# One third of the columns at a time through the first normalisation, and three small reorderings behind it

## What is computed

```python
mix, st = mixer(rmsnorm(x, norm1_w), p, states)   # one input projection w_in, three mixers, gated merge, w_out
x = x + mix
xn = rmsnorm(x, norm2_w)
x = x + square(relu(xn @ w_up)) @ w_down
y = rmsnorm(x, final_norm_w)
def rmsnorm(x, w): return x * rsqrt(mean(x * x, -1) + EPS) * w
```

## Time and profile before

| | |
|---|---|
| Median of 3 runs | 2195.5 us (2195.11 to 2198.4) |
| The profiled execution | 2200.46 us, of which 2198.7 us are the span of its instructions |
| TensorE busy | 2166.3 us, 99% of the span |
| VectorE, ScalarE, GpSimd busy | 971.9, 758.2 and 571.2 us |
| DMA | 222 MB, 101 GB/s over the span |

### The profile page before, as it was taken

How to read it: one execution, slowest core, us unless ns; L and a number is a source line. 1 busy time by engine, 2 the same in 40 slices (tenths; PEclk the granted TensorE clock), 3 DMA queues, 4 the chain that set the end, 5 groups by cost and what they waited for, 6 DMA issues and landing times.

```text
span 2198.7 us, 36263 instructions
## 1 busy us (share of the span) xinstructions
PE 2166.3 (99%) x13762; PEld 2104.9 (96%) x13762; DVE 971.9 (44%) x1522; ACT 758.2 (34%) x1342; POOL 571.2 (26%) x375
## 2 busy tenths in 40 slices
PE   7999999999999999999999999999999999999998
PEld 6999999999899999899998999999999999999997
DVE  5888323333665664244445365442222222222225
ACT  5556323232465563233332333231312213122132
POOL 2438623323211212212212222212221221212120
PEclk9999999999999999999999999999999999999999
DMA  4224536442244323456431744202111111111112
GB/s 173 67 80 135 162 114 188 128 133 89 83 125 144 99 97 118 128 161 193 143 109 59 254 148 146 97 25 58 29 58 34 52 52 33 57 33 52 52 40 88
DMA packets 191538, 222.09 MB, mean 101 GB/s; under 512 B 38670, under 2 KB 146226, under 8 KB 191334
## 3 DMA queue, kind: packets, MB, share of 16 engines
q1 hardware_dynamic: 164364, 179.81, 27.0%
q10 hardware_dynamic: 27098, 41.23, 5.3%
HBM read 162.22 MB, written 58.77 MB: 101 GB/s over the span
## 4 chain that ended last, share of the span: by engine, by line
PE 79%; issue 8%; POOL 4%; DVE 4%; DMA 2%; ACT 2%; SPq 1%; ACTq 0%; POOLq 0%; DVEq 0%
PE D L432 65%; PE D L2811 2%; POOL w_lo L412 2%; POOL b_t L738 1%; POOL b_u L735 1%; DVE u_x L546 1%; PE MM L1302 1%; PE MM L1890 1%; DMA proj<-stage 0%; PE MM L2367 0%; PE MB L1974 0%; PE MM L872 0%; PE MB L2284 0%; PE D L2367 0%; PE MB L2234 0%
## 5 line engine op out<-in xcount | busy, mean ns | idle before, releaser
L432 PE MATMUL D<-xn_hi,w_hi 128*128 128x352 f32 x1992 | 663.7, 333 | 7.3 <-ACT stage L451 2.8
L412 POOL TENSOR_TENSOR w_lo<-w_raw,w_hi 128x1024 fp32r<-128x1024 f32 (+1 forms) x163 | 338.7, 2078 | 1184.7 <-ACT w_hi L406 1184.7
L432 PE MATMUL D<-xn_lo,w_hi 128*128 128x352 f32 x1992 | 644.2, 323 | 0.0
L432 PE MATMUL D<-xn_hi,w_lo 128*128 128x352 f32 x1992 | 643.9, 323 | 0.0
L432 PEld LDWEIGHTS D<-xn_hi,w_hi 128*128 128x128 f32 x1992 | 375.7, 189 | 22.5 <-issue 12.8
L432 PEld LDWEIGHTS D<-xn_lo,w_hi 128*128 128x128 f32 x1992 | 375.8, 189 | 4.7 <-issue 3.8
L432 PEld LDWEIGHTS D<-xn_hi,w_lo 128*128 128x128 f32 x1992 | 375.5, 189 | 0.0
L406 ACT ACTIVATE w_hi<-w_raw 128x1024 fp32r<-128x1024 f32 (+1 forms) x163 | 143.7, 882 | 346.8 <-PE D L432 296.4
L432 PE MATMUL D<-z_lo,w_hi 128*128 128x352 f32 x768 | 247.9, 323 | 0.0
L432 PE MATMUL D<-z_hi,w_lo 128*128 128x352 f32 x768 | 247.8, 323 | 0.0
L432 PE MATMUL D<-z_hi,w_hi 128*128 128x352 f32 x768 | 247.2, 322 | 0.0
(11 more groups left out here) (557 smaller groups left out, 3066.6 us busy)
## 6 DMA issues: line engine op xcount, KB each, us to landing
w_raw<-in_w_proj SPq DMA_DIRECT2D x73, 512.0 KB, 3.7
proj<-stage ACTq DMA_DIRECT2D x60, 528.0 KB, 3.3
w_raw<-in_w_half SPq DMA_DIRECT2D x72, 256.0 KB, 2.7
w_raw<-in_w_full SPq DMA_DIRECT2D x24, 512.0 KB, 3.6
stage<-proj SPq DMA_DIRECT2D x23, 528.0 KB, 3.6
d_bc<-rowd SPq DMA_DIRECT2D x32, 256.0 KB, 5.7
m_in<-proj SPq DMA_DIRECT2D x32, 256.0 KB, 3.8
f_w<-in_w_full SPq DMA_DIRECT2D x16, 512.0 KB, 3.5
```

What stands on the lines that cost most here:

```text
L412: nc.gpsimd.tensor_tensor(w_lo[t.slot][:, 0:kt, :], raw(t)[0][:, 0:kt * P].rearrange("p (k m) -> p k m", m=P), w_hi[t.slot][:, 0:kt, :].bi ...
L432: last = nc.tensor.matmul(D[b][:, 0:GN], w[t.slot][:, k, :], x, start=(k == 0 and n == 0), stop=(k == kt - 1 and n == 2))
```

## The change

1. `xin` comes by thirds of the columns: for each third four loads of two blocks by 352 columns (352 KB), the weights of tile 0 behind the first third, those of tile 1 behind the second. The squares go into a buffer of their own (`sqs`), 24 of 352 columns in place of 8 of 1056; 12 additions of 352 columns in place of 4 of 1056; 12 totals either way. Those of the first third come first; those of the next third stand between the pieces of this one: on ScalarE two squares behind each of the pieces 0 to 3, the root of the next third behind piece 6, the high part of tile 1's weights behind piece 2; on VectorE an addition behind each of the pieces 1 to 4; on TensorE a total behind the tile-0 matmuls of each of the pieces 2 to 5.
2. The gate rows: `ROW_SLOTS` is `[3, 6, 2, 4, 3]`, ScalarE has the first slot and its evacuations ahead of the first Exp, and evacuates once more ahead of the copies of `tok`.
3. SP into the DeltaNet loop: `stored_all` and `d_z` of chunk 0 go ahead of the `td` stores and the `d_t0`/`d_tt0` loads, and for chunk 1 the four `d_bc` go ahead of the weights of tile 19, `d_qk` and `d_v`.
4. The end: in the last block of each third VectorE adds the square of the block before ahead of the bank, and `SCALED` moves one scaling from step 6 to step 7.

```diff
-        x_ld = [sem(f"x_ld{k}") for k in range(KT)]
+        x_ld = [[sem(f"x_ld{g}{p}") for p in range(KT // 2)] for g in range(TG)]
...
+        SQ_AFTER = {k: (2 * k, 2 * k + 1) for k in range(KT // 2)}
+        ROOT_AFTER, WEIGHTS_AFTER = KT - 2, 2
+        ADD_AFTER = {k + 1: k for k in range(KT // 2)}
+        SUM_AFTER = {k + 2: k for k in range(KT // 2)}
...
+        def first_square(eng, g, k):
+
+            eng.wait_ge(x_ld[g][k // 2], 16)
+            if g:
+                eng.wait_ge(*nm_pe["1"].after(f"p{g - 1}{k // 2}"))
+            eng.activation(sqs[:, k, :], xin[:, k, gcols(g)], ACT.Square).then_inc(*nm_act["1"].step(f"q{g}{k}"))
+
+        def first_add(eng, g, p):
+
+            eng.wait_ge(*nm_act["1"].after(f"q{g}{2 * p + 1}"))
+            eng.tensor_tensor(sqs[:, 2 * p, :], sqs[:, 2 * p, :], sqs[:, 2 * p + 1, :], ALU.add).then_inc(*nm_dve["1"].step(f"a{g}{p}"))
+
+        def first_total(eng, g, p):
+
+            eng.wait_ge(*nm_dve["1"].after(f"a{g}{p}"))
+            eng.matmul(M[g][:, 0:GN], ones, sqs[:, 2 * p, :], start=p == 0, stop=p == KT // 2 - 1).then_inc(*nm_pe["1"].step(f"p{g}{p}"))
...
+                        if t == 0 and k in SUM_AFTER and g + 1 < TG:
+                            first_total(eng, g + 1, SUM_AFTER[k])
...
                 root(0)
                 for i, (g, k) in enumerate(PIECES):
-                    if i in (4, 6):
-                        root(i // 2 - 1)
                     eng.wait_ge(*dve_.after(f"s{i}"))
...
+                    if i == WEIGHTS_AFTER:
+                        make_hi(eng, Tile(1))
+                    if g + 1 < TG:
+                        for x in SQ_AFTER.get(k, ()):
+                            first_square(eng, g + 1, x)
+                        if k == ROOT_AFTER:
+                            root(g + 1)
...
                     if i:
                         low(i - 1)
+                    if k in ADD_AFTER and g + 1 < TG:
+                        first_add(eng, g + 1, ADD_AFTER[k])
...
-            for k in range(KT):
-                if k == KT // 2:
-                    load_w(sp, Tile(0), w_proj[0])
-                sp.dma_start(xin[:, k, :], xT[k]).then_inc(x_ld[k], 16)
-            load_w(sp, Tile(1), w_proj[1])
+            for g in range(TG):
+                for p in range(KT // 2):
+                    src = xT[2 * p:2 * p + 2, :, gcols(g)].rearrange("k p t -> p k t")
+                    sp.dma_start(xin[:, 2 * p:2 * p + 2, gcols(g)], src).then_inc(x_ld[g][p], 16)
+                if g < 2:
+                    load_w(sp, Tile(g), w_proj[g])
...
-        ROW_SLOTS, ML_SLOTS = [9, 2, 4, 3], [3, 3, 3, 3, 3, 3]
+        ROW_SLOTS, ML_SLOTS = [3, 6, 2, 4, 3], [3, 3, 3, 3, 3, 3]
...
             if kind == "act":
+                slot()
+                slot.evacuate()
                 eng.wait_ge(*rw_dve.after("bc"))
...
                 slot()
+                slot.evacuate()
                 eng.wait_ge(*rw_pe.after("tok"))
...
                 if n is not None:
                     gates()
                 else:
+                    stored_all(eng, GD0)
+                    gates()
                     inverse_loads(eng, 3)
                     eng.wait_ge(zeroed, 2)
...
-                if n is None:
-                    stored_all(eng, GD0)
-                    gates()
...
-            chunk_loads(sp, gdn, LOOP_GD, 0, 3)
+            gdn("sp", sp, 0, None, False, between="ahead")
+            load_w(sp, Tile(LOOP_GD + 2), w_proj[LOOP_GD + 2])
+            gdn("sp", sp, 0, lambda: load_w(sp, Tile(LOOP_GD + 3), w_proj[LOOP_GD + 3]), False, between="behind")
+            chunk_loads(sp, gdn, LOOP_GD, 1, 3)
...
-        SCALED = {3: (0,), 4: (1, 2), 5: (3, 4), 6: (5, 6), 7: (7,)}
+        SCALED = {3: (0,), 4: (1, 2), 5: (3, 4), 6: (5,), 7: (6, 7)}
...
+                    if d < KT - 1:
+                        gather()
                     if d:
                         eng.wait_ge(*act_.after(f"q{g}{d - 1}"))
...
+                    if d == KT - 1:
+                        gather()
```

More of the change, by code:

```diff
@@ L1497, in rows @@
             if kind == "pool":
-                for _ in range(4):
+                for _ in range(5):
                     slot()
             if kind == "pe":
+                slot()
                 slot()
@@ L1667, in gdn @@
                 if between != "rest":
-                    for k in range(2):
-                        eng.dma_start(hn(B.qk, k * C4), pcols(GD_TILE + 4 * (1 - k), 4, col0, N)).then_inc(gx_in if sample else gd_in, 16)
+                    if between != "ahead":
+                        for k in range(2):
+                            eng.dma_start(hn(B.qk, k * C4), pcols(GD_TILE + 4 * (1 - k), 4, col0, N)).then_inc(gx_in if sample else gd_in, 16)
                 def token_rows():
@@ L1681, in gdn @@
                         eng.wait_ge(s_, 16 * NCONV // 2)
-                eng.dma_start(hn(B.v), pcols(GD_TILE + 8, 4, col0, N)).then_inc(gx_in if sample else gd_in, 16)
-                if n is not None or sample:
+                if between != "ahead":
+                    eng.dma_start(hn(B.v), pcols(GD_TILE + 8, 4, col0, N)).then_inc(gx_in if sample else gd_in, 16)
+                if (n is not None or sample) and between != "behind":
                     prefetch(eng, None if sample else n, (gd_dve, "ge"))
@@ L1688, in gates @@
                     eng.dma_start(hn(B.z), pcols(GZ_TILE, 4, col0, N)).then_inc(gx_in if sample else gd_z, 16)
+                if between == "ahead":
+                    return
                 if sample:
@@ L2308, in build @@
                   "3": steps("nm3_dve", last_names + " " + " ".join(f"s{TG - 1}{k}" for k in range(KT)))}
[L2309 to L2330, removed]
-                    i.then_inc(*nm_pe["1"].step(f"p{pair}"))
@@ new lines, in build, with gcols @@
+        nm_pe = {"1": steps("nm1_pe", " ".join(f"p{g}{p}" for g in range(TG) for p in range(KT // 2))),
+                 "3": steps("nm3_pe", " ".join(f"s{g}" for g in range(TG)))}
+        def gcols(g):
+            return slice(g * GN, (g + 1) * GN)
+        def first_square(eng, g, k):
[3 more added lines that the diff above has]
+            eng.activation(sqs[:, k, :], xin[:, k, gcols(g)], ACT.Square).then_inc(*nm_act["1"].step(f"q{g}{k}"))
@@ L3156, in _ @@
             dve.wait_ge(*lb_act.after("ln"))
-            for k in range(KT):
-                first_sum("dve", dve, k)
-            norm_scale("dve", dve, "1", xin, nrs[:, :], (nsq[:, :], ntmp[:, :]), PC_N1)
+            for p in range(KT // 2):
+                first_add(dve, 0, p)
+            norm_scale("dve", dve)
             mix_program("dve", dve)
@@ L3172, in _ @@
             pe.wait_ge(const_ld, 32)
-            for k in range(KT):
-                first_sum("pe", pe, k)
+            for p in range(KT // 2):
+                first_total(pe, 0, p)
             mix_program("pe", pe)
```

53 lines of the change are left out of this document (31 added, 22 removed).

## The result

The changed kernel takes **2205.25 us** (median of 7 runs, 2203.24 to 2208.14), the kernel before, run beside it, 2196.35 (median of 7, 2193.69 to 2201.1): a ratio of 1.004, 95% interval 1.0031 to 1.0049, so 8.9 us slower. The forecast was 2197.0 with a range to 2201.0; the result lies 4 us above that range. The profiled execution after took 2205.49 us, close to its median. The one before took 2200.46, 4.1 above its own. Of the 8.9 us between the medians the two profiles can therefore show only 5.0, and the other 3.9 need other executions of the kernel before.

The account below looks back on a forecast made before the run. TensorE, busy 99% of the span, was taken as the bound. Start +0.8, gate rows -1.1, DeltaNet loop +1.8, clock 0 and end 0 sum to +1.5: 2202.0 in the profile's frame, 2197.0 for the median, range 2190.0 to 2201.0.

Parts of the forecast that it names:

- The start, +0.8 expected: Start by thirds: the pair of tiles 0 and 1 ends at 50.9 in place of 50.1; bounds -1.7 and +2.3.
- VectorE's two operations on a piece 0.92: Start, supply of pieces: VectorE needs 0.92 us for its two operations on each piece, from 34 in 15.56.
- an addition adds 0.46: Start, supply of pieces: VectorE's addition adds 0.46 us to four of eight pieces, 1.4 each.
- 0.50 up to the middle: Start: TensorE at half clock up to the middle of the first third, the pair then ending at 50.4.
- the bound of +1.7 in the text: Start: all of the first third at half clock, the pair ending at 51.8, +1.7.
- The gate rows, -1.1 expected: Gate rows: 0.6 of the 0.8 stall and 0.45 of the 1.6 one go; bounds 0 and -2.4.
- The stall at x5: Into the DeltaNet loop: TensorE, ready at 257.91, waits for the last load at 262.5, +4.6.
- The rival in which they issue slowly: Into the DeltaNet loop: eight loads at 1.0 us each, stall 8.3, +5.2, 2200.7 us; chance 0.20 (0.21 by range).
- so -2.8 in full: Into the DeltaNet loop: chunk 1's `d_bc` ahead removes the whole 2.8 us TensorE stall at L451.
- the clock: 0 net: Behind the new x5 stall: same half clock as behind the old stall, which lost 2.7; between -1.0 and +0.7.
- the +1.8 of the text: Into the DeltaNet loop: sum of the price +4.6 at x5 and the gain -2.8 at L451.
- I carry differences over unchanged: Frame: sums made against the profiled 2200.46 us, 5.0 above the median 2195.5, hold for the median too.

Follow-up runs that it names:

- the run with the short pieces: Start alone on the kernel before, with GpSimd's `make_lo` of tiles 0 and 1 cut into eight operations of 128 columns: 2199.39 us, ratio 1.0013.
- three kernels: Start alone on the kernel before, plus `make_lo` cut into eight operations (2199.39 us), plus fill matmuls (2201.36), or plus both (2200.36).
- the fills' kernel: Start alone on the kernel before, plus fill matmuls of 256 columns whose result nobody reads: 2201.36 us, ratio 1.0019.
- another kernel with the same fills: Kernel before plus gate rows, early `d_bc`, and the new start with both cut `make_lo` and fill matmuls: 2197.37 us, ratio 0.9996.

## Why the prediction was wrong, point by point

Two steps failed. Between the two profiles +1.5 was forecast and +5.0 measured, and the start makes 3.1 of the difference: its stream of pieces was laid out without GpSimd and with too little half clock. Between the medians another 3.9 come on top, because a stall and a fall of the clock that the profile before holds were booked as a gain in full.

**The start, +0.8 expected, +3.9 in the trace, 1.8 to 3.1 in time.** The step that failed is the one that laid out the supply of pieces. The first piece was nearly right (14.5, measured 15.34 with one lengthened scaling ahead of it). "VectorE's two operations on a piece 0.92" and "an addition adds 0.46" left out that GpSimd makes the low half of tile 1's weights in just that stretch: one addition took 2.13. From there on the stream was late: the first matmul of piece 5 came at 25.61 (21.8 laid out), the Ln of the second root at 28.26 (22.9), piece 8 at 30.36 (26.7). The kernel before already showed it in miniature. Its addition of squares takes 1.26 alone and 1.62 where it starts beside one `make_lo`, and the next `make_lo`, which starts beside that addition, takes 2.84 in place of 2.48; it was read past because nothing waited there:

```profile
8.25 1.26 DVE L2323 TENSOR_TENSOR nsq<-nsq,ntmp 128x1056 f32<-128x1056 f32 x1 [3.23 <-ACT ntmp L2320]
...
16.70 2.48 POOL L412 TENSOR_TENSOR w_lo<-w_raw,w_hi 128x1024 fp32r<-128x1024 f32 x1 [14.12 <-ACT w_hi L406]
...
18.68 1.62 DVE L2323 TENSOR_TENSOR stage<-stage 128x1056 f32<-128x1056 f32 x1 [1.72 <-ACT stage L2320]
19.68 2.84 POOL L412 TENSOR_TENSOR w_lo<-w_raw,w_hi 128x1024 fp32r<-128x1024 f32 x1 [0.49 <-ACT w_hi L406]
```

The Trainium skill (SBUF — State Buffer, SBUF: two separate sides) says that a VectorE operation with two SBUF inputs and a GpSimd operation that reads SBUF exclude each other for the whole instruction; by that rule, the trace agrees, both for the addition (18.74 to 20.87 beside 18.02 to 20.49) and for the run with the short pieces, and it should have been a term of the sum. The second half of the miss is the clock: "0.50 up to the middle" was taken and the whole first third was at 0.50, which alone was the bound of +1.7 in the text, 51.8. The two lengthened operations hold 0.85 and 1.6 us more; with both the end came to 54.01, beyond the upper bound of +2.3. The 3.9 can't be split between them: the end came 1.8 us earlier with either one taken away, and 1.4 with both.

That a thin stretch is followed by half clock was itself read from a single event. In the six other kernels with the old start the same stretch was as thin, 1.54 to 1.75 us busy of 3.50, and the clock behind it stayed at 1.00. So the fall is an event with a chance. In the kernel with SP's order alone the two stretches read:

```profile
22.60:26.10 3.50, 1.69 (x7) 1.13 (x8) 3.43 (x8) 2.16 (x5) 1.43 (x4) 1.00 0.06 22
26.10:29.50 3.40, 2.78 (x12) 1.62 (x11) 3.40 (x8) 3.09 (x8) 0.00 (x0) 1.00 0.00 0
```

**The gate rows, -1.1 expected, -1.5 in the trace.** The first stall went whole (0.8, where 0.6 was taken), the second lost 0.5 (where 0.45 was). The mechanism and its size held; in time the part alone gave 0 with an interval of 2 us either way, and with the early `d_bc` -2.6. One term was left out of the sum: the clock behind the second stall. Behind the 1.6 us stall it fell for 3.4 us in six of nine profiled executions; behind the shortened one of 1.1 us it stayed at 1.00 in all five. Step x5 came at 256.7 and 256.9 in the two kernels with the new gate rows and the old start, at 257.91 in the profile before, which has no fall there, and at 259.5 to 259.9, waits at x5 taken off, in the four that have the old start and the fall. Whether that is a gain in time isn't shown: the mean granted clock of the twelve executions with the gate rows alone (0.997) is that of the kernel before beside them.

**Into the DeltaNet loop: the price was right, the gain was not.** The stall at x5 was forecast at 4.6, from the store of tile 16 down to the last load, and measured 5.10. Two terms inside it were off and nearly cancel: the `td` stores landed after 4.2 to 4.8 (2.7 to 3.1 taken, from a trace in which they went one at a time), and the eight loads took 3.7 to issue (4.3 taken). The rival in which they issue slowly did not happen. The failed step is "so -2.8 in full", and with it "the clock: 0 net". Both were read from one execution. In the six other profiled kernels with the old order that stall was 0.7, 0.8, 1.1, 1.2, 1.5 and 2.0, and TensorE kept its clock behind it. So the change took away about 1 us there and brought 5.1, with 6.8 us at 0.50 behind it where 1.52 + 3.40 were busy: up to 2.5 lost. That sum, 5.1 + 2.5 - 1, is 6.6, against 6.4 measured for the part alone. Against the profiled execution the same rows give 5.1 + 2.5 - 2.8 - 2.7 = +2.1, so the +1.8 of the text was right in its own frame.

**The end, 0 expected, 0 measured** (1.0001).

**The frame.** "I carry differences over unchanged" is the step that cost the other 3.9. The execution profiled before stood 4.1 us above its median. It held a long stall and a fall of the clock that none of the other profiled kernels with that order had, and a change that removes them gains little against the median. The granted clocks on record bear this out. In the 98 other executions of the kernel before that ran beside the experiments the time goes with the mean granted clock: 2198.6 us on average at 0.996 (38 executions), 2196.7 at 0.997 (32), 2195.2 at 0.998 (25) and 2193.7 at 0.999 (3). The profiled one stands at 0.995, below them all; a part of that is its fall at 26 us, which cost little. All the rows that pointed at them were single events, and the distance of 5.0 between 2200.46 and 2195.5, named in the text, was the hint. In hindsight the sum would be: the profile's excess (2.8 - 1 of stall, 2.7 of clock, together 4.5) off the gain, which gives +6.0, 2201.5, and with the start as measured 2204.6.

**Open.** The lines on the start: three kernels moved the pair's end by 1.4 to 1.8 us and none moved the time by as much as the intervals can tell. Why the fills' kernel was the slowest of them isn't settled. Nor is what SP's order costs beside the rest of the change (9.7 us, and 6.4 alone), or whether the stores landed late because they were issued close together or because `d_z` went just ahead of them.

## What to carry to other kernels

A wait put early in a queue that only issues transfers has to be priced by everything behind it in that queue: here a store to DRAM and the loads that read it back, whose whole chain then hung on one earlier store. Before a stall is booked as a gain, compare the profiled execution with the median, and its mean granted clock with that of other executions: if it stands several microseconds above, some of its stalls and falls of the clock can be its own. Here it was a stall that ended with the landing of a load. When small work is laid between the pieces of a start, look what GpSimd does in those microseconds: here the thinner stream met half clock and a VectorE held up by GpSimd at the same time.

## What the runs showed of the hardware

- A VectorE operation with two SBUF inputs that starts beside a long GpSimd operation ends just behind it: 2.12 and 2.13 us in place of 0.53 (GpSimd 128x1024, 2.47 us; in the changed kernel 0.38 behind its end). Beside 128x128 operations of GpSimd it takes 0.77.
- Two 512 KB stores to DRAM issued 0.55 us apart, with a 256 KB load just ahead, land after 4.2 to 4.8 us; issued 2.2 us apart, without that load, they land after 2.6 to 3.1.
- The same stall does not always bring the same clock. Behind the 1.6 us stall at 72 to 77 us (second of L507) TensorE went to 1.2 GHz for 3.4 us in six of nine profiled executions that have it, and not in that of the kernel before; behind 1.1 us it did so in none of five. Step x5 came at 259.5 and 259.7 in two kernels with the fall that are otherwise the kernel before up to there, and at 257.91 without: 1.6 to 1.8 us. Together with the stall on L451 of 0.7 to 2.8 us that can explain part of the spread of 2193.6 to 2202.3 among executions of one and the same kernel before, whose time rises from 2193.7 to 2198.6 as the mean granted clock falls from 0.999 to 0.996.
- Four fill matmuls of 256 columns behind the first totals (1.89 us) and one behind each of two pieces kept the clock at 1.00 through a stretch in which TensorE was busy 1.20 of 3.40 us; in another kernel with the same fills it fell at 23.3 us. One execution each.
- The granted clock of the table is no guide at the very start. The first four totals of the changed kernel took 4.77 us, 1.2 apiece, while the table gives 1.00 from 6 to 12 us; later a total took 1.38 at 0.50 and 0.75 at 1.00.
